# Stick-breaking steps of a hybrid block on one Trainium2 core: projection tiles placed ahead of the scores

## The chip, the cores and the metric

The kernel runs on one core of a Trainium2 chip. The metric is the device time of one execution, in microseconds (us). The kernel before the change took 1916.91 us, the median of three runs (1907.53 to 1917.92). The execution that was profiled took 1912.39 us.

A core has five engines that run their own instruction streams and meet at semaphores: PE (TensorE, matrix products; "PEld" is its weight loading), DVE (VectorE), ACT (ScalarE), POOL (GpSimd) and SP (SyncE, which here only starts transfers). An engine runs its instructions strictly in order, so an instruction that waits holds up all behind it.

## The reference, cut to what matters

The block normalises x, modulates it, and multiplies it by one wide projection matrix. The columns are split between a retention branch and a stick-breaking attention branch; both are merged, projected, and followed by a squared-ReLU MLP. The change is in the stick-breaking branch:

```python
def stick_breaking(q, k, v):
    scale = SB_DH ** -0.5
    for blk in range(S // SB_BLOCK):
        t0, t1 = blk * SB_BLOCK, (blk + 1) * SB_BLOCK
        z = jnp.einsum('bthd,bshd->bhts', q[:, t0:t1], k[:, :t1]) * scale
        valid = s_idx[None, :] < t_idx[:, None]
        log_1m = jnp.where(valid, -jax.nn.softplus(z), 0.0)
        log_stick = lax.cumsum(log_1m, axis=3, reverse=True) - log_1m
        a = jnp.where(valid, jnp.exp(jax.nn.log_sigmoid(z) + log_stick), 0.0)
        outs.append(jnp.einsum('bhts,bshd->bthd', a, v[:, :t1]))
```

S is 1024 and there are 8 heads of width 64. The kernel computes a as sigmoid(z) times a running product of sigmoid(-z), taken from the right.

## The kernel before, in words

All products are float32, each done as three passes over operands split into a high part (rounded) and a low part (the rest): high x high, high x low, low x high. The block runs in stages: normalisation (to about 74 us), the stick-breaking stage (about 74 to 388 us), gates, retention, merge, output projection and the MLP.

**Steps and units.** The stick-breaking stage is a written-out sequence of 48 steps, U = 0 to 47, in four groups G of 12 (two heads each); k is U modulo 12. A unit is up to four key blocks of 128 for one block of 128 queries (`UNITS`, line 72). Its width w is 128, 256, 384, 512 for k = 0 to 3, then 512 and 128, 512 and 256, 512 and 384, 512 and 512 for k = 4 to 11. Units that hold the diagonal (k = 0, 1, 2, 3, 4, 6, 8, 10) also get a mask product.

**What a unit passes through.** PE makes the scores S(U) (`scores`, lines 575 and 581). ACT makes four sigmoids from them (lines 944, 945: sigmoid(-z) into `uu`, sigmoid(z) into `sg`, for each head). DVE runs one scan for each head over `uu` (1297), at k = 4, 6, 8 and 10 a two-element copy (1300), and one product into `sg` (1303), after which the semaphore `a_done` says that the weights of unit U are ready. PE transposes them, WT(U) (`weights_transposed`, 591), ACT copies the result to `aT` (937), and PE multiplies by the values, V(U) (`times_v`, 608). WT(U) and V(U) stand in step U + 2, so the unit has until then to be ready.

**Tiles beside the steps.** The projections for q, k, v and the first gate columns are tiles 0 to 35 (`STICK_TILE`). Tiles 0 and 1 stand ahead of step 0, the others in steps by the table `STICK_BESIDE` (line 89), whole or in parts of their eight k chunks: a v tile, or half a q, k or gate tile, takes about 3 us. A line of it:

```python
    5: ((10, 0, 4),), 6: ((10, 4, 8),), 7: ((11, 0, 8),), 8: ((12, 0, 4),), 9: ((12, 4, 8),), 10: ((13, 0, 8),),
```

Steps 11, 23, 35 and 47 have no tile. A finished tile is evicted by ACT (`high`, lines 917, 920, 922); for q and k tiles DVE then makes the low part from the bank and the high part (`low`, 1278). A tile waits for the eviction of the tile two before it.

**Order on PE in one step:** WT(U-2), S(U), the tiles of the step, V(U-2). On ACT: the copy of a finished output block, the copy `aT`, the four sigmoids, then `high`. On DVE: scans, product, then `low`.

**Weights.** POOL splits each weight piece into high and low parts, two additions and two subtractions of 128x1024 (lines 410 and 412), into one of two slots. A piece can be split once the last tile that uses the slot's old piece has finished. In this stage these are tile 7 (in step 3), 13 (step 10), 15 (step 14), 23 (step 26), 29 (step 34), 31 (step 38) and 35 (step 46). Tile 16, in step 15, needs the piece whose split starts at the end of tile 15.

Of the kernel before, what the change touches and what calls it, by code (L numbers as in the profile page):

```python
# [12 lines left out]
KC = D // P  # L13
# [65 lines left out]
STICK_TILE = ([("q", 0, 0), ("k", 0, 0)] +  # L79
              [("v", 0, t) for t in range(4)] + [("q", 0, 1), ("k", 0, 1), ("v", 0, 4), ("v", 0, 5), ("q", 1, 0), ("v", 0, 6), ("k", 1, 0), ("v", 0, 7)] +  # L80
              [("q", 1, 1), ("k", 1, 1), ("v", 1, 0), ("q", 2, 0), ("v", 1, 1), ("k", 2, 0), ("v", 1, 2), ("v", 1, 3)] +
              [("q", 2, 1), ("k", 2, 1), ("v", 1, 4), ("v", 1, 5), ("q", 3, 0), ("v", 1, 6), ("k", 3, 0), ("v", 1, 7)] +
              [("q", 3, 1), ("k", 3, 1)] + [("a", 0, j) for j in range(4)])
# [62 lines left out]
def build_block(nc, x, wstream, ada, ada_rows, smalls, pos, ident, maskd, dprime, adab, postg, out, m1_dram, mods, x2_dram):  # L146
# [4 lines left out]
    with ctx:  # L151
# [3 lines left out]
        def sb(name, shape, dt, c=ctx):  # L155
            return c.enter_context(nc.sbuf_tensor(name, shape, dt))
# [65 lines left out]
        with ExitStack() as c:  # L222
            r_hi = sb("r_hi", [P, KC, S], f32r, c)
            r_lo = sb("r_lo", [P, KC, S], f32r, c)
            with ExitStack() as c2:
                qk = sb("qk", [P, T, 256], f32, c2)
# [265 lines left out]
        def _(pe):  # L492
# [63 lines left out]
            def passes(outp, hi, lo, r_hi_, r_lo_, start, stop):  # L556

                nc.tensor.matmul(outp, hi, r_hi_, start=start, stop=False)  # L558
                nc.tensor.matmul(outp, hi, r_lo_, start=False, stop=False)  # L559
                return nc.tensor.matmul(outp, lo, r_hi_, start=False, stop=stop)  # L560
# [22 lines left out]
            def weights_transposed(U):  # L583

                _, b0, b1, _ = UNITS[U % N_UNITS]
                pe.wait_ge(a_done, U + 1)
                if U:
                    pe.wait_ge(at_ready, U)
                for h in range(2):
                    for b in range(b1 - b0):  # L590
                        last = nc.tensor.transpose(px[:, h, b * P:(b + 1) * P], sg[:, U % 2, h, b * P:(b + 1) * P], id_f[:, :])  # L591
                last.then_inc(at_tr, 1)
# [21 lines left out]
            def stick_tile(n, k0=0, k1=KC):  # L614

                kind, at, tok = STICK_TILE[n]
                piece = 3 * (at // 2) + 2 * (at % 2) if kind in "qk" else 3 * at + 1 if kind == "v" else PC_GATE
                slot = piece % 2
                if k0 == 0:
                    pe.wait_ge(w_split, 4 * piece + 4)  # L620
                    if n == 0:
                        pe.wait_ge(n1_split, 16)
                    if n == TILE_AT["q", 0, 1]:
                        pe.wait_ge(n1_split, 32)
                    if n >= 4:
                        pe.wait_ge(*((ev_act, EA_STICK + n - 1) if STICK_TILE[n - 2][0] in "va" else (qk_low, LOW_AFTER[n - 1])))
                for k in range(k0, k1):
                    if kind == "v":
                        l, r_ = ((a[:, k, tok * P:(tok + 1) * P] for a in (a_hi, a_lo)), (w[:, slot, k * 256:(k + 1) * 256] for w in (w_hi, w_lo)))
                    else:  # L630
                        m, th = ("qk".index(kind), tok) if kind in "qk" else TT[tok]
                        l, r_ = ((w[:, slot, k * 256 + m * P:k * 256 + (m + 1) * P] for w in (w_hi, w_lo)),
                                 (a[:, k, th * HALF:(th + 1) * HALF] for a in (a_hi, a_lo)))
                    last = passes(tile_bank(n)[:, 0:256 if kind == "v" else HALF], *l, *r_, k == 0, k == KC - 1)
                if k1 == KC:
                    last.then_inc(gemm_done, 1)
# [3 lines left out]
            for U in range(ALL_UNITS + 2):  # L640
                if U >= 2:
                    weights_transposed(U - 2)
                if U < ALL_UNITS:
                    scores(U)
                for n, k0, k1 in STICK_BESIDE.get(U, ()):
                    stick_tile(n, k0, k1)
                if U >= 2:
                    times_v(U - 2)

# [7 lines left out]
            for g in range(GATE_G):  # L657
                ea, ev = EA_GATE + 8 * g, EV_GATE + 8 * g
                n = PC_GATE + 3 * g
# [225 lines left out]
        def _(act):  # L885
# [25 lines left out]
            def high(n):  # L911

                kind, at, tok = STICK_TILE[n]
                bank = tile_bank(n)
                act.wait_ge(gemm_done, TL_STICK + n + 1)
                if kind == "v":
                    nc.scalar.activation(vs[:, at, tok, :, :].rearrange("p a d -> p (a d)"), bank[:, 0:256], ACT.Copy).then_inc(ev_act, 1)
                elif kind == "a":
                    m, th = TT[tok]
                    nc.scalar.activation(m1s[:, m, th * HALF:(th + 1) * HALF], bank, ACT.Sigmoid).then_inc(ev_act, 1)  # L920
                else:
                    nc.scalar.activation(qk_hi[at % 2][:, "qk".index(kind), tok * HALF:(tok + 1) * HALF], bank, ACT.Copy,
                                         scale=SB_DH ** -0.5 if kind == "q" else 1.0).then_inc(ev_act, 1)
# [3 lines left out]
            for U in range(ALL_UNITS + 3):  # L927
                if U >= 3 and (U - 3) % N_UNITS in LAST_UNIT:
                    G, k = divmod(U - 3, N_UNITS)
                    i = UNITS[k][0]  # L930
                    act.wait_ge(av_done, T * G + i + 1)
                    nc.scalar.activation(sbt_f[:, G, i * P:(i + 1) * P], px[:, 2, 0:P], ACT.Copy).then_inc(sbt_ready, 1)
                if 2 <= U < ALL_UNITS + 2:
                    _, b0, b1, _ = UNITS[(U - 2) % N_UNITS]
                    w = (b1 - b0) * P
                    act.wait_ge(at_tr, U - 1)
                    nc.scalar.activation(aT[:, :, 0:w], px[:, 0:2, 0:w], ACT.Copy).then_inc(at_ready, 1)
                if U < ALL_UNITS:
                    _, b0, b1, _ = UNITS[U % N_UNITS]
                    w = (b1 - b0) * P  # L940
                    for h in range(2):
                        z = z_bank(2 * U + h, w)
                        act.wait_ge(z_done, 2 * U + h + 1)
                        nc.scalar.activation(uu[:, U % 2, h, HALF - w:HALF], z, ACT.Sigmoid, scale=-1.0).then_inc(sg_done, 1)  # L944
                        nc.scalar.activation(sg[:, U % 2, h, 0:w], z, ACT.Sigmoid).then_inc(sg_done, 1)
                for n, _, k1 in STICK_BESIDE.get(U, ()):
                    if k1 == KC:
                        high(n)

            def row_out(v):  # L950

# [253 lines left out]
        def _(dve):  # L1205
# [67 lines left out]
            def low(n):  # L1273

                kind, at, tok = STICK_TILE[n]
                m, cols = "qk".index(kind), slice(tok * HALF, (tok + 1) * HALF)
                dve.wait_ge(ev_act, EA_STICK + n + 1)
                V.scalar_tensor_tensor(qk_lo[at % 2][:, m, cols], tile_bank(n), 1.0 if m else SB_DH ** -0.5,
                                       qk_hi[at % 2][:, m, cols].bitcast(f32), ALU.mult, ALU.subtract).then_inc(qk_low, 1)
# [4 lines left out]
            for U in range(ALL_UNITS):  # L1284
                G, k = divmod(U, N_UNITS)
                _, b0, b1, diagonal = UNITS[k]
                w, slot = (b1 - b0) * P, U % 2
                pad = uu[:, slot, :, HALF:HALF + 1]
                if k == 1 and G:
                    V.memset(pad, 1.0).then_inc(pad_set, 1)  # L1290
                    pads += 1
                if pads:
                    dve.wait_ge(pad_set, pads)
                for h in range(2):
                    run = uu[:, slot, h, HALF - w:HALF if diagonal else HALF + 1][:, ::-1]
                    dve.wait_ge(sg_done, 4 * U + 2 * h + 1)
                    V.tensor_tensor_scan(run, run, run, 1.0, ALU.mult, ALU.bypass).then_inc(scan_done, 1)  # L1297
                dve.wait_ge(scan_done, 2 * U + 2)
                if k not in LAST_UNIT:
                    V.tensor_copy(uu[:, 1, :, HALF:HALF + 1], uu[:, 0, :, 0:1]).then_inc(pad_set, 1)  # L1300
                    pads += 1
                dve.wait_ge(sg_done, 4 * U + 4)
                V.tensor_tensor(sg[:, slot, :, 0:w], sg[:, slot, :, 0:w], uu[:, slot, :, HALF - w + 1:HALF + 1], ALU.mult).then_inc(a_done, 1)
                for n, _, k1 in STICK_BESIDE.get(U, ()):
                    if k1 == KC and STICK_TILE[n][0] in "qk":
                        low(n)


            dve.wait_ge(sbt_ready, 4 * T)
# [401 lines left out]
```

## Time and profile before

| | |
|---|---|
| median of three runs | 1916.91 us |
| profiled execution, time / span | 1912.39 / 1910.6 us |
| PE busy, share of the span | 1752.6 us, 92% |
| DVE busy | 952.9 us, 50% |
| ACT busy | 534.9 us, 28% |
| POOL busy | 667.9 us, 35% |
| PE in the chain that ended last | 82% |

The span is the time from the first to the last instruction of the profiled execution. Busy time is what an engine's instructions cover. The chain that ended last is followed back from the last instruction through what released each one. In rows of the trace, times are us from the start of the span; "[idle before <-X]" gives how long the engine stood idle ahead of a row and what ended it. "x8" is a number of merged instructions. The 48 steps cover 87 to 388 us. Where a matmul's bar overlaps the next one's, starts are what is to be read, since the ends are modelled.

### The profile page before, as it was taken

The numbers are of one execution on the slowest core, as the hardware profiler recorded it, in microseconds if no ns is written. First come the engines' busy times: TensorE is split into PE (matmuls) and PEld (weight loads), VectorE is DVE, ScalarE is ACT, GpSimd is POOL, SyncE is SP. The second block draws the span as 40 slices with busy tenths as digits, with TensorE's granted clock in tenths as the row PEclk, the third lists the DMA queues.
The fourth block names the chain that finished last, engine by engine and source line by source line (L and its number), as shares of the span: only waits on it lengthen the run. The fifth ranks groups of instructions, "written<-read, shape, count | busy, mean of one in ns | idle before, by whom it ended". The sixth has DMA issues, their size and how long they took to land.

```text
span 1910.6 us, 24819 instructions
## 1 busy us (share of the span) xinstructions
PE 1752.6 (92%) x9648; PEld 1449.9 (76%) x9648; DVE 952.9 (50%) x1291; ACT 534.9 (28%) x918; POOL 667.9 (35%) x282
## 2 busy tenths in 40 slices
PE   1697999899899989999999995789999999999998
PEld 1585777677698979897888895568888888888876
DVE  6647566766544554544111547464526345351616
ACT  3344454501012121211000233232333323233332
POOL 3014023214322313131334685055354444535320
PEclk8799999989899999999999997899999999999999
DMA  8001001146321111110311444111112021111213
GB/s 323 12 23 34 12 23 34 45 144 220 99 103 45 37 37 34 37 44 24 132 44 44 144 155 154 56 44 45 52 36 76 23 77 33 55 44 44 67 39 138
DMA packets 38076, 135.11 MB, mean 71 GB/s; under 512 B 5860, under 2 KB 6756, under 8 KB 37480
## 3 DMA queue, kind: packets, MB, share of 16 engines
q1 hardware_dynamic: 30304, 109.27, 17.1%
q10 hardware_dynamic: 7688, 24.67, 3.5%
q8 instruction: 59, 0.97, 0.2%
q14 instruction: 25, 0.20, 0.0%
HBM read 121.33 MB, written 12.60 MB: 70 GB/s over the span
## 4 chain that ended last, share of the span: by engine, by line
PE 82%; DVE 10%; issue 3%; POOL 2%; ACT 1%; DMA 0%; POOLq 0%; DVEq 0%; SPq 0%; ACTq 0%
PE ps L497 15%; PE ps L499 15%; PE ps L498 15%; PE ps L829 5%; PE ps L831 5%; PE ps L830 5%; PE ps L558 3%; PE ps L559 2%; PE ps L560 2%; PE ps L591 2%; PE ps L575 2%; PE ps L608 2%; PE ps L708 1%; DVE sg L1258 1%; DVE qk L1424 1%
## 5 line engine op out<-in xcount | busy, mean ns | idle before, releaser
L410 POOL TENSOR_TENSOR w_hi<-raw,zero 128x1024 fp32r<-128x1024 f32 x80 | 165.2, 2065 | 771.4 <-PE ps L499 371.0
L497 PE MATMUL ps<-r_hi,w_hi 128*128 128x512 f32 x640 | 253.6, 396 | 23.0 <-issue 20.3
L499 PE MATMUL ps<-r_hi,w_lo 128*128 128x512 f32 x640 | 254.9, 398 | 0.0
L498 PE MATMUL ps<-r_lo,w_hi 128*128 128x512 f32 x640 | 253.9, 397 | 0.0
L497 PE MATMUL ps<-w_hi,a_hi 128*128 128x256 f32 x768 | 225.4, 293 | 16.9 <-DVE qkT L1430 8.9
L499 PE MATMUL ps<-w_hi,a_lo 128*128 128x256 f32 x768 | 220.4, 287 | 0.0
L498 PE MATMUL ps<-w_lo,a_hi 128*128 128x256 f32 x768 | 220.3, 287 | 0.0
L412 POOL TENSOR_TENSOR w_lo<-raw,w_hi 128x1024 fp32r<-128x1024 f32 x80 | 210.6, 2632 | 6.3
L436 POOL TENSOR_TENSOR w_lo<-w,w_hi 128x1024 fp32r<-128x1024 f32 x39 | 99.6, 2553 | 251.6 <-ACT w_hi L1091 251.6
L1564 DVE TENSOR_TENSOR m<-m,ps 128x512 f32<-128x512 f32 x224 | 146.2, 682 | 71.3 <-PE ps L831 70.8
L497 PEld LDWEIGHTS ps<-w_hi,a_hi 128*128 128x128 f32 x768 | 150.1, 195 | 21.1 <-POOL w_hi L410 10.1
L829 PE MATMUL ps<-w_hi,f_hi 128*128 128x512 f32 x392 | 156.3, 399 | 5.8 <-issue 4.7
L497 PEld LDWEIGHTS ps<-r_hi,w_hi 128*128 128x128 f32 x640 | 120.9, 189 | 52.6 <-issue 20.5
L1297 DVE TENSOR_TENSOR_SCAN uu<-uu 128x512 f32<-128x512 f32 (+7 forms) x96 | 108.9, 1175 | 100.0 <-ACT uu L944 100.0
L830 PE MATMUL ps<-w_lo,f_hi 128*128 128x512 f32 x392 | 155.9, 398 | 0.0
L831 PE MATMUL ps<-w_hi,f_lo 128*128 128x512 f32 x392 | 155.9, 398 | 0.0
L498 PEld LDWEIGHTS ps<-w_lo,a_hi 128*128 128x128 f32 x768 | 150.2, 196 | 0.0
L499 PEld LDWEIGHTS ps<-w_hi,a_lo 128*128 128x128 f32 x768 | 149.8, 195 | 0.0
L498 PEld LDWEIGHTS ps<-r_lo,w_hi 128*128 128x128 f32 x640 | 120.9, 189 | 30.2
L499 PEld LDWEIGHTS ps<-r_hi,w_lo 128*128 128x128 f32 x640 | 121.0, 189 | 28.9
L1557 DVE TENSOR_TENSOR f_lo<-hid,f_hi 128x1024 fp32r<-128x1024 f32 x35 | 51.7, 1478 | 150.2 <-ACT f_hi L1118 150.2
L436 POOL TENSOR_TENSOR w_lo<-raw,w_hi 128x1024 fp32r<-128x1024 f32 x32 | 77.6, 2432 | 102.0 <-ACT w_hi L1091 101.6
(224 smaller groups left out, 3369.4 us busy)
## 6 DMA issues: line engine op xcount, KB each, us to landing
raw<-wstream SPq DMA_DIRECT2D x112, 512.0 KB, 3.6
ada_r<-ada_rows SPq DMA_DIRECT2D x32, 512.0 KB, 4.6
w<-wstream SPq DMA_DIRECT2D x32, 512.0 KB, 3.5
ada_s<-ada SPq DMA_DIRECT2D x8, 1024.0 KB, 18.5
xs<-x SPq DMA_DIRECT2D x2, 2048.0 KB, 11.0
m_dram<-m1s ACTq DMA_DIRECT2D x1, 4096.0 KB, 13.0
m<-m_dram ACTq DMA_DIRECT2D x1, 4096.0 KB, 12.5
x_dram<-m ACTq DMA_DIRECT2D x8, 512.0 KB, 2.9
```

Of the source, the lines that this page charges most:

```text
L410: nc.gpsimd.tensor_tensor(w_hi[:, slot, part], raw[:, h, :], zero[:, 0:1].broadcast_to([P, RAW]), ALU.add).then_inc(w_split, 1)
L412: nc.gpsimd.tensor_tensor(w_lo[:, slot, part], raw[:, h, :], w_hi[:, slot, part].bitcast(f32), ALU.subtract).then_inc(w_split, 1)
L436: return nc.gpsimd.tensor_tensor(out_, in0, in1, op)
L497: nc.tensor.matmul(outp, lh, rh, start=(k == 0), stop=False)
L498: nc.tensor.matmul(outp, lh, rl, start=False, stop=False)
L499: last = nc.tensor.matmul(outp, ll, rh, start=False, stop=(k == chunks - 1))
L558: nc.tensor.matmul(outp, hi, r_hi_, start=start, stop=False)
L829: nc.tensor.matmul(banks[:, t, :], fh, wh, start=(start and c == 0), stop=False, skip_group_check=not start)
L830: nc.tensor.matmul(banks[:, t, :], fh, wl, start=False, stop=False, skip_group_check=not start)
L831: last = nc.tensor.matmul(banks[:, t, :], fl, wh, start=False, stop=(c == 1), skip_group_check=not start)
L1297: V.tensor_tensor_scan(run, run, run, 1.0, ALU.mult, ALU.bypass).then_inc(scan_done, 1)
L1564: V.tensor_tensor(dst, dst, bank, op).then_inc(ff_ev, 1)
```

## The change

In each step, PE now runs the step's tiles ahead of the scores instead of behind them; ACT evicts a finished tile ahead of the step's sigmoids; DVE makes the low part of a q or k tile ahead of the step's scans. Nothing else is changed: the table, the buffers, the waits and the number of instructions are the same. Lines below the edits shift by three on DVE (1297 is 1300 after the change, 1303 is 1306, while 1278 stays) and on ACT (944 is 947, 945 is 948).

```diff
             for U in range(ALL_UNITS + 2):
                 if U >= 2:
                     weights_transposed(U - 2)
+                for n, k0, k1 in STICK_BESIDE.get(U, ()):
+                    stick_tile(n, k0, k1)
                 if U < ALL_UNITS:
                     scores(U)
-                for n, k0, k1 in STICK_BESIDE.get(U, ()):
-                    stick_tile(n, k0, k1)
                 if U >= 2:
                     times_v(U - 2)
...
                     nc.scalar.activation(aT[:, :, 0:w], px[:, 0:2, 0:w], ACT.Copy).then_inc(at_ready, 1)
+                for n, _, k1 in STICK_BESIDE.get(U, ()):
+                    if k1 == KC:
+                        high(n)
                 if U < ALL_UNITS:
...
                         nc.scalar.activation(sg[:, U % 2, h, 0:w], z, ACT.Sigmoid).then_inc(sg_done, 1)
-                for n, _, k1 in STICK_BESIDE.get(U, ()):
-                    if k1 == KC:
-                        high(n)
...
                 _, b0, b1, diagonal = UNITS[k]
+                for n, _, k1 in STICK_BESIDE.get(U, ()):
+                    if k1 == KC and STICK_TILE[n][0] in "qk":
+                        low(n)
...
                 V.tensor_tensor(sg[:, slot, :, 0:w], sg[:, slot, :, 0:w], uu[:, slot, :, HALF - w + 1:HALF + 1], ALU.mult).then_inc(a_done, 1)
-                for n, _, k1 in STICK_BESIDE.get(U, ()):
-                    if k1 == KC and STICK_TILE[n][0] in "qk":
-                        low(n)
```

PE in step 10, before the change, from WT(8) to the start of step 11: L591 are the transposes of the weights, L575 and L581 the scores of unit 10 with their mask, L558 the first pass of each k chunk of tile 13, L608 the product with v.

```order
L591 MATMUL ps<-id_f,sg 128x128 [waits at_ready,a_done]
...
L575 MATMUL ps<-qk_hi0 128x512 [waits sg_done]
...
L581 MATMUL ps<-msk_b,id_b 128x128 x2
L558 MATMUL ps<-w_hi,a_hi 128x256 [waits ev_act,w_split]
...
L608 MATMUL ps<-aT,vs 64x128 [waits sbt_ready,ev_act,at_ready]
L608 MATMUL ps<-aT,vs 64x128 x7
```

The same step after the change:

```order
L591 MATMUL ps<-id_f,sg 128x128 [waits at_ready,a_done]
...
L558 MATMUL ps<-w_hi,a_hi 128x256 [waits ev_act,w_split]
...
L575 MATMUL ps<-qk_hi0 128x512 [waits sg_done]
...
L581 MATMUL ps<-msk_b,id_b 128x128 x2
L608 MATMUL ps<-aT,vs 64x128 [waits sbt_ready,ev_act,at_ready]
L608 MATMUL ps<-aT,vs 64x128 x7
```

The scores have moved behind the 24 matmuls of the tile, and nothing stands between them and V(8) now.

DVE in steps 9 and 10 before the change, from the first scan of unit 9 (384 wide, with one carried element) to the product of unit 10; L1278 is the low part of tile 12, a k tile that ends in step 9.

```order
L1297 SCALAR_TENSOR_TENSOR uu<-uu 128x385 [waits sg_done,pad_set]
L1297 SCALAR_TENSOR_TENSOR uu<-uu 128x385 [waits sg_done]
L1303 TENSOR_TENSOR sg<-sg,uu 128x2x384 [waits sg_done,scan_done]
L1278 SCALAR_TENSOR_TENSOR qk_lo<-ps,qk_hi 128x512 [waits ev_act]
L1297 SCALAR_TENSOR_TENSOR uu<-uu 128x512 [waits sg_done,pad_set]
L1297 SCALAR_TENSOR_TENSOR uu<-uu 128x512 [waits sg_done]
L1300 COPY uu<-uu 128x2 [waits scan_done]
L1303 TENSOR_TENSOR sg<-sg,uu 128x1024 [waits sg_done]
```

The same place after the change:

```order
L1278 SCALAR_TENSOR_TENSOR qk_lo<-ps,qk_hi 128x512 [waits ev_act]
L1300 SCALAR_TENSOR_TENSOR uu<-uu 128x385 [waits sg_done,pad_set]
L1300 SCALAR_TENSOR_TENSOR uu<-uu 128x385 [waits sg_done]
L1306 TENSOR_TENSOR sg<-sg,uu 128x2x384 [waits sg_done,scan_done]
L1300 SCALAR_TENSOR_TENSOR uu<-uu 128x512 [waits sg_done,pad_set]
L1300 SCALAR_TENSOR_TENSOR uu<-uu 128x512 [waits sg_done]
L1303 COPY uu<-uu 128x2 [waits scan_done]
L1306 TENSOR_TENSOR sg<-sg,uu 128x1024 [waits sg_done]
```

The low part has moved from behind the product of unit 9 to ahead of its scans.

## Rows read from the trace of the kernel before

**Rows 1.** Waits of PE, 86 to 392 us: total us, times, longest us.

```profile
PE ps L591 <- DVE sg L1303: 11.6, 5, 5.4
PE ps L558 <- POOL w_lo L412: 8.4, 1, 8.4
PE ps L608 <- ACT aT L937: 2.4, 2, 1.3
PE ps L575 <- DVE qk_lo L1278: 1.4, 1, 1.4
```

**Rows 2.** Windows, a stretch without long waits: length, busy us, PE clock, DMA.

```profile
240.00:300.00 60.00, 59.50 (x444) 46.30 (x443) 37.74 (x43) 31.89 (x71) 10.26 (x4) 1.00 0.06 19
```

**Rows 3.** Chain, steps 22 to 24: S(22), V(20), WT(22); start us, us.

```profile
231.51 0.90 PE ps L575 x4
...
235.49 1.02 PE ps L608 x16
...
239.10 1.02 PE ps L591 x8
```

**Rows 4.** Chain: the scores S(16), 512 wide.

```profile
198.92 0.89 PE ps L575 x6
```

**Rows 5.** Timeline of DVE behind these scores: start us, us, instruction, idle before.

```profile
200.71 2.34 DVE L1297 TENSOR_TENSOR_SCAN uu<-uu 128x512 f32<-128x512 f32 x2 [7.45 <-ACT uu L944]
...
203.16 1.22 DVE L1303 TENSOR_TENSOR sg<-sg,uu 128x1024 f32<-128x1024 f32 x1
```

**Rows 6.** Timeline of POOL: weight splits after tiles 7, 13, 23 and 35.

```profile
115.00 1.89 POOL L410 TENSOR_TENSOR w_hi<-raw,zero 128x1024 fp32r<-128x1024 f32 x1 [64.13 <-PE ps L560]
...
155.87 1.89 POOL L410 TENSOR_TENSOR w_hi<-raw,zero 128x1024 fp32r<-128x1024 f32 x1 [31.43 <-PE ps L560]
157.84 3.30 POOL L412 TENSOR_TENSOR w_lo<-raw,w_hi 128x1024 fp32r<-128x1024 f32 x1
161.10 2.81 POOL L410 TENSOR_TENSOR w_hi<-raw,zero 128x1024 fp32r<-128x1024 f32 x1
163.99 3.15 POOL L412 TENSOR_TENSOR w_lo<-raw,w_hi 128x1024 fp32r<-128x1024 f32 x1
...
257.43 1.89 POOL L410 TENSOR_TENSOR w_hi<-raw,zero 128x1024 fp32r<-128x1024 f32 x1 [65.25 <-PE ps L560]
...
370.40 1.90 POOL L410 TENSOR_TENSOR w_hi<-raw,zero 128x1024 fp32r<-128x1024 f32 x1 [33.07 <-PE ps L560]
```

**Rows 7.** Timeline of DVE during the split after tile 13.

```profile
155.93 1.85 DVE L1300 COPY uu<-uu 128x2 f32<-128x2 f32 x1
157.70 1.21 DVE L1303 TENSOR_TENSOR sg<-sg,uu 128x1024 f32<-128x1024 f32 x1
159.24 5.75 DVE L1297 TENSOR_TENSOR_SCAN uu<-uu 128x513 f32<-128x513 f32 x2 [0.33 <-ACT uu L944]
165.03 3.19 DVE L1303 TENSOR_TENSOR sg<-sg,uu 128x1024 f32<-128x1024 f32 x1
```

**Rows 8.** Chain: WT(3), WT(11), WT(27), and the first gate matmul.

```profile
123.96 1.02 PE ps L591 x8
...
168.27 1.09 PE ps L591 x8
...
268.99 1.09 PE ps L591 x8
...
387.85 0.73 PE ps L497
```

**Rows 9.** Windows around waits of PE: the granted clock is third from the end.

```profile
170.00:172.00 2.00, 2.00 (x7) 1.61 (x6) 1.20 (x2) 1.53 (x5) 0.00 (x0) 0.50 0.03 12
172.00:174.00 2.00, 2.00 (x8) 1.58 (x7) 0.77 (x2) 0.14 (x1) 0.00 (x0) 0.69 0.00 0
...
194.00:196.00 2.00, 2.00 (x11) 2.00 (x11) 0.00 (x0) 0.00 (x0) 0.00 (x0) 0.50 0.43 174
...
270.00:272.00 2.00, 2.00 (x13) 1.65 (x13) 1.97 (x4) 1.70 (x5) 0.00 (x0) 1.00 0.30 121
```

## The prediction

> **What bounds the kernel now.** I read the waits of PE in the stick-breaking stage first, then one quiet stretch, then the chain and the timelines of DVE and POOL around the longest waits. In the quiet stretch PE is busy 59.5 of 60 us at full clock, DVE 37.7 and ACT 31.9 [rows 2]: PE's own work sets the pace, and reordering gains nothing there unless a handover gets shorter. All of PE's other time is in four kinds of wait [rows 1]: 11.6 us for unit weights (`a_done`), 8.4 us once for a weight split, 2.4 us for the copy `aT`, and 1.4 us ahead of S(0) for the low part of tile 1. So the change can win at most 23.8 us here, and the question is what it does to each.
>
> The largest kind is made by POOL. Unhindered, scores that start at 198.92 have their first scan at 200.71 and the product's end at 204.38: 1.8 us and 5.5 us after the start of S [rows 4, 5]. During a split it is another picture [rows 6, 7]. A two-element copy takes 1.85 us and ends with POOL's first operation. POOL's next one takes 3.30 us, and it ends 2.2 us after DVE's product has ended (158.91 to 161.14). The second scan ends at 164.99, 1.1 us after POOL's third operation (163.91); the last product ends at 168.22, 1.1 us after the fourth (167.14). The two engines take turns, operation by operation: 1.9 and 2.2 us for POOL, 1.1 to 1.2 us for a 512-wide scan or product.
>
> Read instead as plain slowing (5.75 + 3.19 us for what takes 2.34 + 1.22), unit 10 below would be ready at T+10.7 and not T+9.5, and each of six events dearer by up to 1.2 us; I go by turns, and this is in the range.
>
> The Trainium skill (SBUF — State Buffer, section "SBUF: two separate sides") says of these two engines that the port pair they share is an exclusive lock, kept for a whole instruction, and no split of bandwidth. By that rule the sum is the one below, by plain slowing some 7 us more. The trace agrees with the rule: the waits end where the other engine's operations end.
>
> **The change part by part.** It removes and adds no instruction and no DMA; POOL's and SP's orders stay. What changes is distance. WT(U) needs the product of unit U. Before, S(U) had its own tile, V(U-2), WT(U-1), S(U+1), the tile of step U+1 and V(U-1) behind it to cover its 5.5 us. Now its own tile is ahead of it, so the cover is one tile, about 3.0 us, shorter: V(20) starts 4.0 us after S(22), 1.0 of scores and 3.0 of tile [rows 3]. Second, a split starts when a tile ends. Before, the scores of that step were already out by then; now the scores come after, so all DVE work of that unit falls into the split. T is the end of the tile that lets a split start; the new T is earlier than the old by the scores that moved behind it (1.0 us for 512 wide, 0.8 for 384).
>
> *Quiet steps.* With a tile in the next step the cover is 6.3 us or more (for k = 6: 1.0 + 1.0 + 0.4 + 3.0 + 0.5 + 0.4, phase lengths scaled from [rows 3] by the number of blocks), against 5.5: nothing is lost. Unit 22 has no tile in step 23. From S(22) to WT(22) are 7.6 us now, of which the tile was 3.0 [rows 3]; left are 4.6 against 5.5, so +0.9 us. Units 10, 34 and 46 have no such tile either, but meet a split.
>
> *Split after tile 13 (T = 155.8), unit 10.* S(10) starts at T, its scan is ready at T+1.8, and POOL's first operation ends at T+2.0 [rows 6]. By turns: scan to 3.1, POOL to 5.3, scan to 6.4, POOL to 8.3, copy and product to 9.5, POOL to 11.7. PE has only 4.6 us of work (same widths as unit 22), so WT(10) waits 4.9 us. Then WT(10), five chunks of tile 14, S(12), V(10) are 1.0 + 3.7 + 0.6 + 1.1 = 6.4, and WT(11) starts at T+15.9; the product of unit 11 ends at 11.7 + 1.1 + 1.2 + 1.2 = T+15.2, in time. The new T is 1.0 earlier: 14.9, against 168.27 - 155.8 = 12.5 now [rows 8]. That is +2.4. The split after tile 29 (unit 34) has the same widths: +2.4.
>
> *Splits after tiles 23 and 31 (T = 257.35), units 26 and 38, 384 wide.* Scan and product cost 0.9 (three quarters of [rows 5]): 2.0, 2.9, 5.1, 6.0, 7.9, product at T+8.8. PE has 0.8 + 0.4 + 0.6 + 3.0 + 1.0 + 0.6 = 6.4, so it waits 2.4. Then 5.6 more to WT(27), T+14.4, less 0.8 is 13.6, against 268.99 - 257.35 = 11.6 now [rows 8]: +2.0 each.
>
> *Split after tile 7 (T = 114.95), unit 3.* Tile 8 still stands between, so the scan is ready at T+4.8. POOL ends its third operation at 6.2 first; scan 7.3, POOL 9.5, scan 10.6, product 11.8 (POOL is done). Less 1.0 is 10.8, against 123.96 - 114.95 = 9.0 [rows 8]: +1.8, with 1.7 us idle.
>
> *Split after tile 15.* Tile 16 waits for it before and after [rows 1]. Before, S(14) and S(15) were both out ahead of that wait; now only S(14) is, and S(15) (1.0) stands behind tile 16. One more DVE operation gets in among POOL's (0.9), and the start is 0.8 earlier: +1.0 rounded.
>
> *End, split after tile 35 (T = 370.3), units 46 and 47.* As for unit 10, the product of 46 is at T+9.5 and that of 47 at T+15.2. WT(47) at the low clock 2.0, `aT` 1.1, V(47) 2.0 give T+20.3, less 1.0 is 19.3, against 387.85 - 370.3 = 17.5 [rows 8]: +1.8.
>
> *Start.* Tiles 2 and 3 now stand where PE waited for the low part of tile 1: -1.4 [rows 1]. `high` and `low` ahead of sigmoids and scans cost nothing: they run (0.6 and 0.7 us on ACT and DVE, estimated from the 128x512 scan and product of [rows 5]) while PE makes the scores that the sigmoids wait for. Without that cover each would cost its own length in a step that waits, 6 x 0.7 = 4.2 us at most, which I keep for the range.
>
> *Clock.* After the wait of 2.58 us that ends with WT(11) at 168.27 the granted clock is 0.50 and then 0.69 in the next windows, 1.2 instead of 2.4 GHz for some 3 us: about 1.5 us lost. After the 8.4 us wait it is 0.50 still two to four us on. After the 0.5 us wait ahead of WT(27) it stays 1.00 [rows 9]. So the two 2.4 us waits add 1.5 each; the 4.9 us waits of units 10 and 34 add 2.0 where 1.5 is paid already, +0.5 each; the 1.7 us wait of unit 3 lies between 0 and 1.5, and I take 0. Clock: +4.0.
>
> *Handovers.* PE changes kind of work four times a step before and after, but tile to scores and scores to V are pairs that the quiet trace hardly shows. Over 44 steps with a tile, bounds are -0.1 and +0.1 us a step, -4.4 and +4.4; I take 0, since each of the present four handovers costs about the same.
>
> Sum: 0.9 + 2.4 + 2.4 + 2.0 + 2.0 + 1.8 + 1.0 + 1.8 - 1.4 + 4.0 = +16.9 us. All later stages start from the end of this one and are untouched, so it reaches the end. The profiled execution took 1912.4 us: 1929.3. The median of the three runs is 4.5 us higher; from it the sum gives 1933.8. I say 1932.
>
> **Rivals.**
> *Relocation only.* POOL's and DVE's work during a split is fixed, so the new wait at unit U may just replace the old one at U+1, and each event costs only the moved scores. For it: after the first unit the next one's product (T+15.2) does come in time. Against: PE's remaining work behind WT(10) is 6.4 us, and it can't run during the wait. It would give about 6 x 1.0 + 0.9 - 1.4 = +5.5, 1921.
> *More clock and dearer handovers.* If the clock falls after the 1.7 us wait too (+1.5), if the handovers cost 0.1 more (+4.4) and `high` and `low` delay the sigmoids (+4.2): +27, 1942. For it: scores use half of the array's rows, and leaving a tile for them is a change of shape; against: nothing in the trace shows a dear one.
> *Faster, by the handovers.* If V right behind the scores, and the tile right behind the transposes, start without a gap, a quiet step gets shorter. The chip would have to give back over 16.9 / 44 = 0.38 us a step to break even, and 0.6 to be 0.5% faster. With half of the 1.0 us of the scores hidden, 0.5 a step, it is -22 + 16.9 = -5, 1910. Against: PE is busy 59.5 of 60 us in such steps [rows 2].
>
> **How the numbers follow.** The forecast has 0.68, relocation 0.14, the dearer case 0.13, the faster one 0.05. The forecast's own range is 1925 to 1939: the handovers' bounds and 3 us of spread between runs. To hold 8 in 10 the range goes from 1921 to 1941. This kernel's measurement tells about 0.5%, 9.6 us, from no change, so slower begins at 1926.5. The forecast puts nearly all of its chance there, the dearer case all, relocation a little: slower 0.83. Same is most of relocation, part of the faster case and the low end of the forecast: 0.14. Faster 0.03.
>
> **What would show it.** In the changed profile the waits of PE for the product (now line 1306) should be about 25 us in seven or eight waits instead of five: near 4.9 at WT(10) and WT(34), 2.4 at WT(26) and WT(38), 1.7 at WT(3), 0.9 at WT(22), and those at WT(11) and WT(35) gone. The wait for the low part ahead of S(0) should be gone, the one for the split of tile 16 about 9 us. The first gate matmul should start near 388 + 17 = 405 us. Clock windows of 0.50 should follow four waits that have none now or a shorter one. I am wrong if WT(10) waits under 3 us, if a quiet step is over 0.1 us longer or shorter than now, or if a stage after the first gate matmul differs by over 2 us in length.

## The result and the profile after

The changed kernel takes 1917.85 us, the median of 20 runs (1915.67 to 1920.13). The kernel before, now with 20 runs, the three from before the change among them, takes 1909.28 us (1902.99 to 1917.92). The ratio is 1.004, with a 95% interval of 1.0028 to 1.0053: slower by 8.6 us, clear of no change but under the 9.6 us from which I had called a result slower. I had forecast 1932 us in a range of 1921 to 1941. The measured time lies 3 us below that range: the sign was right, the shift of the stage was forecast twice too large (16.9 us against 8.0).

The waits of PE in the stage, changed kernel (total us, times, longest us), to be set against [rows 1]:

```profile
PE ps L591 <- DVE sg L1306: 20.2, 8, 4.4
PE ps L558 <- POOL w_lo L412: 8.6, 1, 8.6
PE ps L608 <- ACT aT L937: 2.2, 2, 1.1
```

The waits for unit weights grew from 11.6 us in five to 20.2 us in eight; the wait ahead of S(0) is gone; that for tile 16 is as before. PE's timeline in the changed kernel shows where the eight lie (start us, us, instruction, idle before): WT(3), WT(10), WT(22), WT(26), WT(34), WT(38), WT(46) and WT(47).

```profile
124.22 1.09 PE L591 MATMUL ps<-id_f,sg 128*128 128x128 f32 x8 [1.80 <-DVE sg L1306]
...
163.42 1.97 PE L591 MATMUL ps<-id_f,sg 128*128 128x128 f32 x8 [4.39 <-DVE sg L1306]
...
240.47 1.09 PE L591 MATMUL ps<-id_f,sg 128*128 128x128 f32 x8 [0.72 <-DVE sg L1306]
...
266.02 0.87 PE L591 MATMUL ps<-id_f,sg 128*128 128x128 f32 x6 [1.89 <-DVE sg L1306]
...
310.92 1.97 PE L591 MATMUL ps<-id_f,sg 128*128 128x128 f32 x8 [4.39 <-DVE sg L1306]
...
339.10 0.87 PE L591 MATMUL ps<-id_f,sg 128*128 128x128 f32 x6 [1.95 <-DVE sg L1306]
...
385.30 1.97 PE L591 MATMUL ps<-id_f,sg 128*128 128x128 f32 x8 [4.40 <-DVE sg L1306]
...
390.97 1.97 PE L591 MATMUL ps<-id_f,sg 128*128 128x128 f32 x8 [0.61 <-DVE sg L1306]
```

Before the change the five waits were at WT(11) and WT(35) (2.6 us each), WT(27) and WT(39) (0.5 each) and WT(47) (5.4). At unit 22 no split runs, and the scans are as short as ever; only the cover is shorter. In the other places a split runs, and a scan starts only when POOL's operation has ended. The timelines of POOL and DVE in the changed kernel during the split after tile 13, to be set against [rows 6, 7]:

```profile
154.31 1.89 POOL L410 TENSOR_TENSOR w_hi<-raw,zero 128x1024 fp32r<-128x1024 f32 x1 [32.48 <-PE ps L560]
156.28 3.17 POOL L412 TENSOR_TENSOR w_lo<-raw,w_hi 128x1024 fp32r<-128x1024 f32 x1
159.41 2.81 POOL L410 TENSOR_TENSOR w_hi<-raw,zero 128x1024 fp32r<-128x1024 f32 x1
162.29 3.29 POOL L412 TENSOR_TENSOR w_lo<-raw,w_hi 128x1024 fp32r<-128x1024 f32 x1
```

```profile
156.03 4.50 DVE L1300 TENSOR_TENSOR_SCAN uu<-uu 128x512 f32<-128x512 f32 x2 [2.84 <-ACT uu L947]
160.56 1.68 DVE L1303 COPY uu<-uu 128x2 f32<-128x2 f32 x1
162.15 1.21 DVE L1306 TENSOR_TENSOR sg<-sg,uu 128x1024 f32<-128x1024 f32 x1
```

The whole DVE work of unit 10 now lies in the split, operation against operation: scans done at 160.53, POOL's third operation at 162.22, copy behind it, product at 163.36. The tile had ended at 154.2, so the product is ready 9.2 us later; I had worked out 9.5.

**Where the time went.** When WT(U-2) starts in step U, PE has done the same work in both orders, so the starts in the two timelines can be subtracted. The first tile starts 0.1 us later in the changed kernel, which is taken off in the first line.

| stretch | measured shift, us | forecast, us |
|---|---|---|
| start, to WT(0) (100.21 to 98.80) | -1.5 | -1.4 |
| split after tile 7, to WT(3) | +1.9 | +1.8 |
| split after tile 13, WT(9) to WT(12) | +1.6 | +2.9 |
| split after tile 15 | +0.1 | +1.0 |
| unit 22 | +0.9 | +0.9 |
| split after tile 23, WT(25) to WT(27) | +1.5 | +3.5 |
| split after tile 29, WT(33) to WT(36) | +3.0 | +2.9 |
| split after tile 31, WT(37) to WT(39) | +2.9 | +3.5 |
| end, WT(45) to the first gate matmul | +1.3 | +1.8 |
| all other steps | -3.5 | 0 |
| first gate matmul, 387.8 to 396.0 | +8.2; without the late start +8.0 | +16.9 |

The shift of the stage, 8.0 us, accounts for nearly all of the difference of the medians (8.6). The two profiled spans differ by only 3.5 us, and this needs a word. Retention, between the first and the last of its gate matmuls, took 315.0 us in the profiled execution of before and 311.6 in that of the changed kernel (window, length, busy us, clock), before and after:

```profile
569.10:884.10 315.00, 299.98 (x2049) 269.58 (x2048) 154.78 (x410) 54.65 (x118) 84.06 (x40) 0.97 0.11 36
```

```profile
576.30:887.90 311.60, 296.43 (x2049) 266.01 (x2048) 154.78 (x410) 54.68 (x118) 84.07 (x40) 0.98 0.12 36
```

DVE, ACT and POOL do the same in both, PE has as many instructions, and the clock was 0.01 lower. I take that for chance of a run and not for the change: in twelve of the fourteen profiles below that stretch took 311.0 to 311.7 us, in the old and in the new order of the stage alike; the other two, both with a new order on PE, took 312.3 and 314.7.

### The profile page after: what moved, and what is told of

Same layout as the page of the kernel before. It is cut to its first block, busy times and chain, and to the rows that moved or that the text cites. A ratio compares the mean times of both kernels' runs of the same rounds, so it can differ in the third digit from the quotient of the medians.

```text
span 1914.1 us, 24819 instructions
## 1 busy us (share of the span) xinstructions
PE 1748.2 (91%) x9648; PEld 1449.0 (76%) x9648; DVE 952.0 (50%) x1291; ACT 531.6 (28%) x918; POOL 667.8 (35%) x282
## 4 chain that ended last, share of the span: by engine, by line
PE 81%; DVE 11%; issue 3%; POOL 2%; ACT 1%; DMA 0%; POOLq 0%; DVEq 0%; SPq 0%; ACTq 0%
PE ps L497 15%; PE ps L498 15%; PE ps L499 15%; PE ps L829 5%; PE ps L831 5%; PE ps L830 5%; PE ps L558 3%; PE ps L559 3%; PE ps L560 3%; PE ps L591 2%; DVE uu L1300 2%; PE ps L575 1%; PE ps L608 1%; PE ps L708 1%; DVE sg L1258 1%
## 5 line engine op out<-in xcount | busy, mean ns | idle before, releaser
L497 PE MATMUL ps<-r_hi,w_hi 128*128 128x512 f32 x640 | 253.0, 395 | 22.8 <-issue 20.2
L1300 DVE TENSOR_TENSOR_SCAN uu<-uu 128x512 f32<-128x512 f32 (+7 forms) x96 | 115.1, 1240 | 81.9 <-ACT uu L947 81.5
```

The lines of the kernel that those rows point to most:

```text
L497: nc.tensor.matmul(outp, lh, rh, start=(k == 0), stop=False)
```

## The experiments

Each kernel is timed beside the kernel before on the same chip. The shift given is that of the first gate matmul against 387.8 us. It is read from one profiled execution of each kernel and holds the chance of its start: where the clock was low during the first tiles, at 74 to 78 us, all that follows came up to 1.3 us later.

**The new order in the quiet steps, and in the split steps.** A set of steps selects the order in all three streams:

```diff
+SPLIT_STEPS = (3, 10, 14, 22, 26, 34, 38, 46)
...
-                for n, k0, k1 in STICK_BESIDE.get(U, ()):
-                    stick_tile(n, k0, k1)
+                if U not in SPLIT_STEPS:
+                    for n, k0, k1 in STICK_BESIDE.get(U, ()):
+                        stick_tile(n, k0, k1)
                 if U < ALL_UNITS:
                     scores(U)
+                if not (U not in SPLIT_STEPS):
+                    for n, k0, k1 in STICK_BESIDE.get(U, ()):
+                        stick_tile(n, k0, k1)
```

The second run has `U in SPLIT_STEPS` in its place. ACT's and DVE's streams are edited in the same way.

> The new order in all steps except 3, 10, 14, 22, 26, 34, 38 and 46 (those where a weight split starts, and 22, whose next step has no tile), which keep the old order. Theory A (the loss is made in the split steps by the shorter cover, while all other steps gain about 0.1 us each by cheaper handovers and the start 1.5 us): none of the new waits, first gate matmul 1.5 + 36 x 0.1 = 5 us earlier than before, near 383 us, and the time 0.2 to 0.3% under before. Rival B (the new order costs in every step, the waits only happen to lie in the split steps): first gate matmul at or after 388 us, time 0 to 0.3% over before.

> The complement: the new order only in steps 3, 10, 14, 22, 26, 34, 38 and 46. Theory A: all of the new waits (20 us for the product instead of 11.6), no start gain, nearly no handover gain: first gate matmul 12 to 13 us later than before, near 400 us, time 0.6 to 0.7% over before, that is over the changed kernel too. Rival B: under half of that, 4 us or less. If the two parts are independent, the shifts of this run and of the run with the other steps add up to the 8.2 us of the full change.

Measured: quiet steps only, 1903.71 us, ratio 0.9974 (0.9957 to 0.9991), shift -3.3. Split steps only, 1921.57 us, ratio 1.0072 (1.005 to 1.0094), shift +15.4. The waits of PE for the product, quiet and split:

```profile
PE ps L592 <- DVE sg L1317: 12.6, 5, 5.4
```

```profile
PE ps L592 <- DVE sg L1317: 20.0, 8, 4.4
```

The loss is made in eight steps, and the other 36 with a tile bring time: 3.3 us, where I had said 5. The two shifts add to 12.1, not 8.2. Two parts of the difference can be named: their starts to WT(0) are 1.7 us later together than that of the full change, by the clock of the first tiles; and in the split-steps run the clock fell behind the wait of WT(26), which cost 2.9 us where the full change lost 1.5:

```profile
270.00:272.00 2.00, 1.12 (x6) 0.84 (x6) 2.00 (x2) 0.00 (x0) 1.92 (x2) 0.81 0.16 64
272.00:274.00 2.00, 2.00 (x10) 1.21 (x10) 2.00 (x1) 0.86 (x2) 1.04 (x1) 0.50 0.00 0
```

**POOL taken out of the stage, both orders.** The splits of pieces 2 to 8 cover 32 columns in place of 1024. These two kernels leave out the other columns of those weights' high and low parts, so they do not compute the block; they show only what the time is without POOL's work.

```diff
-                    part = slice(h * RAW, (h + 1) * RAW)
+                    part = slice(h * RAW, h * RAW + width)
...
-                piece(n, n + 1, n % 2, TL_STICK + TILE_AT[last] + 1)
+                piece(n, n + 1, n % 2, TL_STICK + TILE_AT[last] + 1, 32)
```

> Old order, but the weight splits of pieces 2 to 8 cover 32 of 1024 columns only (the low and high parts of those pieces are left out otherwise), so POOL is gone from the stage while all semaphores stay. Theory A: the waits of PE for the product and for the split vanish (11.6 and 8.4 us), the low clock behind them too (some 5 us): first gate matmul near 361 to 365 us. Rival B (the scans are slow by themselves, POOL has little to do with it): the waits for the product stay over 5 us.

> New order with the same narrow splits. Theory A: without POOL the shorter cover costs only 0.9 us each at units 10, 22, 34 and 46, against 1.5 us at the start and 0.1 us a step of handovers: first gate matmul 1 to 3 us earlier than in the old order with narrow splits, so that the sign of the change turns. Rival B (the order itself costs): 3 us or more later.

Measured: old order 1880.58 us, shift -26.6; new order 1877.45 us, shift -28.5. Without the splits the new order is 1.9 us earlier, 1.5 of them at the start: the sign of the change turns. The old order has no wait for the product left (its 2.4 us for `aT` and 1.4 us ahead of S(0) stay); the new one has five short ones:

```profile
PE ps L591 <- DVE sg L1306: 3.1, 5, 0.7
```

So the splits cost this stage 26.6 us in the old order, most of it in the two kinds of wait of [rows 1] that are gone (11.6 and 8.4 us), the rest in the low clock behind them: PE's busy time in the stage fell from 278.0 to 271.2 us, with the clock at 1.00 and not 0.96.

**The low clock behind a wait.** The changed kernel with unused matmuls ahead of WT(10) and WT(34). The line left out waits until the bank that they write is free:

```diff
+                if U in (12, 36):
...
+                    for _ in range(18):
+                        nc.tensor.matmul(tile_bank(14), a_hi[:, 0, 0:P], a_hi[:, 0, 0:HALF], start=True, stop=True)
                 if U >= 2:
                     weights_transposed(U - 2)
```

> The changed kernel with 18 unused matmuls (128x512, into the free bank of the next tile) ahead of WT(10) and ahead of WT(34), where PE waits 4.4 us. Theory A (part of what a wait costs is the low clock after it): the granted clock stays at 1.00 through both places, WT and the tile behind it take 0.85 and 3.7 us instead of 1.6 and 4.3 to 5.5, and the first gate matmul comes 3 to 4 us earlier than in the changed kernel, near 392 us. Rival B (the clock follows something else): no change, or 1 us later.

Measured: 1912.16 us, ratio 1.0019 (0.9998 to 1.0041), shift +5.3, 2.8 less than the changed kernel. From WT(9) to WT(12) it lost 0.3 us and not 1.6, from WT(33) to WT(36) 0.3 and not 3.0: 4.0 us in these two places; 1.3 were lost at the start of the stage, before the first edit, by the clock of the first tiles. Windows behind WT(10), in the changed kernel and in this one:

```profile
163.00:165.00 2.00, 1.58 (x8) 1.58 (x9) 2.00 (x2) 0.00 (x0) 2.00 (x1) 0.51 0.00 0
165.00:167.00 2.00, 2.00 (x8) 1.63 (x7) 2.00 (x2) 1.02 (x1) 0.58 (x1) 0.64 0.24 29
```

```profile
164.00:166.00 2.00, 1.90 (x13) 1.39 (x13) 2.00 (x2) 0.10 (x1) 2.00 (x1) 1.00 0.00 0
166.00:168.00 2.00, 2.00 (x10) 1.62 (x9) 2.00 (x2) 0.92 (x1) 0.95 (x1) 1.00 0.11 12
```

WT(10) came as long after WT(9) as in the changed kernel (to 0.03 us); only the clock held. Theory A stands, with 4.0 us in the two places where I had said 3 to 4.

**The two halves of the change apart.**

> Only PE's part of the change: tiles ahead of scores, while ACT evicts behind the sigmoids and DVE makes low parts behind the product, as before. Theory A: as the changed kernel, except that the low part of tile 7 now stands behind the product of unit 3, which the split delays, and S(4) waits for it, about 3 us more: first gate matmul near 399 us. Rival C (evicting ahead of the sigmoids is what costs in the changed kernel): 3 us or more earlier than the changed kernel.

> Only the part of ACT and DVE: the tile stands behind the scores on PE as before, but is evicted ahead of the sigmoids. Theory A: the sigmoids of a step in which a tile ends now wait for its end, so the cover is a tile shorter as in the changed kernel, with none of its gains at the handovers: waits of PE for the product 20 to 27 us, first gate matmul 12 to 17 us later than before. Rival C: as before within 2 us.

The first has only the first hunk of the diff, the second only the others. Measured: PE's part alone 1929.2 us, ratio 1.0109 (1.0072 to 1.0145), shift +18.6; ACT's and DVE's part alone 1940.58 us, ratio 1.0169 (1.0132 to 1.0207), shift +30.9. Waits of PE in the first:

```profile
PE ps L591 <- DVE sg L1307: 17.0, 7, 4.1
...
PE ps L558 <- DVE qk_lo L1282: 7.2, 1, 7.2
```

and in the second:

```profile
PE ps L591 <- DVE sg L1312: 23.5, 8, 5.2
...
PE ps L575 <- ACT sg L949: 5.8, 9, 2.2
```

Both directions were right and both shifts too small: I had said some 11 us and 12 to 17. In the first it was not S(4) that waited for the low part of tile 7 but tile 9, which needs the bank of tile 7 and now stands ahead of S(4): 7.2 us, where I had said 3. PE also waited 2.6 us for evictions of v tiles. In the second, PE also waited for the sigmoids themselves, 5.8 us, which I had left out: they free the banks of the scores. The largest part that I had left out is the clock. Windows of the stage, before and in the second kernel:

```profile
86.00:387.80 301.80, 277.97 (x2033) 216.61 (x2033) 182.34 (x178) 142.66 (x307) 73.25 (x28) 0.96 0.08 27
```

```profile
86.00:418.60 332.60, 289.50 (x2038) 224.51 (x2036) 182.57 (x178) 135.47 (x307) 74.25 (x28) 0.92 0.07 25
```

PE is busy 11.5 us longer with the same work, at a clock of 0.92 (third from the end) and not 0.96; in the changed kernel it was 0.7 us longer, at 0.94.

Rival C is out: with tiles ahead on PE, evicting ahead of the sigmoids saves time.

**A third order: the scores first.**

```diff
+                if U == 0:
+                    for n, k0, k1 in STICK_BESIDE[0]:
+                        stick_tile(n, k0, k1)
+                if U < ALL_UNITS:
+                    scores(U)
                 if U >= 2:
                     weights_transposed(U - 2)
-                if U < ALL_UNITS:
-                    scores(U)
...
```

The part left out keeps step 0's tiles from standing twice on PE, and moves ACT's eviction of tiles 2 and 3 ahead of the sigmoids of unit 0. In the second run the scores stand first only in steps with a tile.

> A third order: S(U), WT(U-2), tile, V(U-2), with tiles 2 and 3 ahead of S(0); ACT and DVE as before. Theory A: the product has two tiles of cover again (5.5 us and about 5.6 us to spare with the sigmoids behind the copy aT), so the waits in the split steps are those of before, while the pair transposes to tile and the start keep their gain: first gate matmul 4 to 5 us earlier than before, near 383 us, time 0.2 to 0.3% under before. Rival D (the handover gain belongs to scores directly ahead of V): first gate matmul at 386 to 388 us.

> As the run with the scores first, but in the steps without a tile (11, 23, 35, 47) PE keeps transposes, scores, product with v. Theory A: the waits for the copy aT in those steps go (about 1.1 us each), all else stays: first gate matmul 6 to 9 us earlier than before, time 0.3 to 0.4% under before. Rival: the waits only change their name, within 1 us of the run with scores first.

Measured: 1904.12 us, ratio 0.9984 (0.9965 to 1.0002), shift -5.3; and 1904.81 us, ratio 0.9981 (0.9963 to 1.0), shift -7.0. The waits for the product are 9.9 and 12.2 us, about as before the change (11.6); those for `aT` fell from 5.9 to 2.2 by the second edit. The stage moved as theory A has it, and rival D (386 to 388 us) is out, the first gate matmul being at 382.5; the times can't tell these two from the kernel before with certainty, nor from each other.

**Shorter splits.** ACT makes the high parts of pieces 2 to 8 behind the sigmoids and `high`, POOL only the low parts.

```diff
+            def weights_high(n, last):
+                act.wait_ge(gemm_done, TL_STICK + last + 1)
+                for h in range(2):
+                    act.wait_ge(raw_full[h], 16 * (n + 1))
+                    nc.scalar.activation(w_hi[:, n % 2, h * RAW:(h + 1) * RAW], raw[:, h, :], ACT.Copy).then_inc(w_act, 1)
...
+                if U in WEIGHTS_AT:
+                    weights_high(*WEIGHTS_AT[U])
```

> Old order, but ACT makes the high parts of weight pieces 2 to 8, so that POOL has only the two subtractions left in each split. Theory A: a split takes some 6.5 us instead of 11.3, so the wait for tile 16 falls from 8.4 to about 4 us and the waits for the product by more than half, the low clock with them: first gate matmul 10 to 14 us earlier than before. Rival (ACT is then late with its sigmoids, 2 us of added work in such a step): 5 us or less.

> The changed kernel's order with the same shorter splits. Theory A (the sign of the change depends on the length of the splits, which its shorter cover meets): the 8.2 us by which it is later now shrink to between 0 and 4 us against the old order with the same splits. Rival B: 8 us as before.

Measured: old order 1892.77 us, ratio 0.9925 (0.9901 to 0.9948), shift -14.3. New order 1906.92 us, ratio 0.9981 (0.9959 to 1.0003), shift -4.9. The old order did nearly as expected: one wait for the product of 2.3 us is left, and tile 16 waits 5.3, where I had said 4. The new order stays 9.5 us behind it, where I had said 0 to 4: rival B's number came (8), and what the new order costs did not shrink with the splits. Its waits:

```profile
PE ps L566 <- POOL w_lo L408: 9.5, 2, 7.0
PE ps L616 <- ACT aT L952: 8.1, 5, 2.0
PE ps L599 <- DVE sg L1323: 4.1, 5, 2.1
```

In the old order with the same splits these are 5.3, 3.5 and 2.3 us. The three together are 10.6 us longer in the new order; less the wait of 1.4 us at the start, that is 9.2 of the 9.5. My reason for it was that ACT's high parts stood behind sigmoids that now come late. The next run moves them ahead of the sigmoids:

> The changed order with ACT's high parts of the weights directly behind the eviction of the tile, ahead of the step's sigmoids, and not behind them as in the run before. Theory A (in that run the high parts stood behind sigmoids that now wait for the later scores, so each split began some 3 us late and tile 16 waited 7.0 us instead of 5.3): the splits start at the tile's end again, the wait for tile 16 is 5 us or less, the one of 2.5 us for the piece of tile 10 goes, and the first gate matmul comes 3 to 7 us earlier than in that run, 7 to 12 us before that of the unchanged kernel. Rival (the shorter cover itself costs as much with shorter splits): within 2 us of that run, and the time moves into waits for the product, over 8 us of them.

Measured: 1916.14 us, ratio 1.0045 (1.0024 to 1.0065), shift +12.5. The first half came true, the second didn't:

```profile
PE ps L599 <- DVE sg L1323: 19.3, 7, 3.7
PE ps L566 <- POOL w_lo L408: 5.2, 1, 5.2
```

The splits began in time and the waits of tiles for them fell from 9.5 to 5.2 us, but ACT's two operations now delay the sigmoids of seven units and come back as waits for the product. Neither theory had this right: in the new order nothing is left in a split step to hide about 2 us on ACT, ahead of the sigmoids or behind them. That this alone makes the 9.5 us is argued, not shown; with the splits taken out altogether, and ACT's work as it was, the new order was the earlier one.

**The best versions.**

> Scores first in steps with a tile, together with ACT's high parts. Theory A: the two gains add up: first gate matmul 16 to 22 us earlier than before, time 0.8 to 1.2% under before. Rival: ACT's added work delays the sigmoids, which already stand behind the copy aT here, and under 12 us are left.

> New order except in steps 3, 10, 14, 22, 26, 34, 38 and 46, with ACT's high parts behind the sigmoids. Theory A: the gain of that order (3.3 us with a start 0.4 us late) and that of the shorter splits (14.3 us) add up: first gate matmul 17 to 19 us earlier than before, time 0.8 to 1.1% under before. Rival: ACT's added work in a step with the eviction elsewhere delays the copy aT, 14 us or less.

Measured: scores first with ACT's high parts 1892.68 us, ratio 0.9916 (0.9888 to 0.9943), shift -19.6; the new order in the quiet steps, the old one in the split steps, with ACT's high parts 1890.62 us, ratio 0.9904 (0.9877 to 0.9931), shift -18.9. Waits of the latter:

```profile
PE ps L567 <- POOL w_lo L409: 5.5, 1, 5.5
PE ps L617 <- ACT aT L957: 3.5, 5, 1.1
PE ps L600 <- DVE sg L1334: 2.3, 1, 2.3
```

Both beat the kernel before and the changed one, and in the second the gains add up to within 1.3 us: -14.3 and -3.3 give -17.6, against -18.9. Against the old order with ACT's high parts alone (1892.77 us) the stage is 5.3 and 4.6 us shorter, but the times, 0.1 and 2.2 us lower with ranges that overlap, don't show it with certainty.

## Why the prediction was right in sign and wrong in size

The mechanism held and the sum did not: it gave +16.9 us where the stage moved by 8.0. The step that failed is the sizing of its terms: the handovers, put at nothing, were -3.5 us; the waits behind the splits were 3.1 us shorter than worked out; the clock was 1.3 and the split after tile 15 was 0.9 less than charged. By the bound that I had set, 9.6 us from no change, the measured 8.6 us counts as "same", to which I had given 0.14, and not as "slower", to which I had given 0.83.

*The cover.* Right. A unit's own tile left its cover, the waits appeared at the units that were named, WT(11) and WT(35) lost theirs, and without splits the change gains (the narrow pair). What the shorter cover costs with half-length splits I had wrong (the 9.5 us above).

*Turns between POOL and DVE.* Right. The product of unit 10 was due 9.5 us after the tile and came at 9.2. Plain slowing would have given 10.7. The waits of 4.9, 2.4, 1.7 and, without a split, 0.9 were 4.4, 1.9, 1.8 and 0.7.

*Handovers, set to 0 between -4.4 and +4.4.* This is the largest term that failed: -3.5 us over the other steps. The chain of the kernel before shows V(14), WT(15), S(17), tile, V(15):

```profile
202.88 0.81 PE ps L608 x12
203.69 1.02 PE ps L591 x8
204.71 0.48 PE ps L575 x6
205.19 0.44 PE ps L558
...
208.21 1.02 PE ps L608 x16
```

and that of the changed kernel V(14), WT(15), tile, S(17), V(15):

```profile
204.10 0.81 PE ps L608 x12
204.91 1.02 PE ps L591 x8
...
208.73 0.48 PE ps L575 x6
209.21 1.02 PE ps L608 x16
```

The same work takes 5.33 us before and 5.11 after. In the timelines the eight transposes hand over after 1.02 us to scores and after 0.85 us to a tile. Scores with a mask ahead of V take 1.12 us where they took 1.00 ahead of a tile, so a step with a 512-wide diagonal unit gains nearly nothing and one without a mask 0.2. I had taken 0 because the four present handovers cost about the same; the new pairs don't. The bound of -4.4 held it, the value I chose did not.

*The clock, set to +4.0.* Behind the waits of WT(10) and WT(34) the tile took 4.3 and 5.5 us in place of 3.7; behind WT(26) nothing was lost, behind WT(38) 1.5. Windows of the changed kernel:

```profile
266.00:268.00 2.00, 1.98 (x17) 1.98 (x18) 2.00 (x1) 0.81 (x1) 2.00 (x1) 1.00 0.00 0
268.00:270.00 2.00, 2.00 (x17) 1.84 (x18) 2.00 (x2) 0.21 (x1) 0.20 (x1) 1.00 0.40 70
...
341.00:343.00 2.00, 2.00 (x6) 1.57 (x5) 2.00 (x2) 0.00 (x0) 0.27 (x1) 0.50 0.28 63
```

Two waits of 1.9 us with the same kinds of work in front, one with the clock at 1.00 behind it and one at 0.50. (Behind the first stands a v tile, behind the second half a gate tile; but behind the first the clock fell as well in the split-steps run.) I had charged 1.5 to each. Net of what before paid, the clock cost about 2.7 us (-0.1, +1.3 and +1.5), 1.3 less than forecast.

*The split after tile 15, set to +1.0.* It cost 0.1. I had added a third DVE operation of 0.9 us to POOL's turns; the split took 10.3 us in both kernels, since the 384-wide operations that meet it now are shorter than the 512-wide ones that met it before.

*Shorter waits than worked out* make up the rest: 0.5 to 0.7 us in each of five splits, 3.1 us together, the cheaper handovers within them included. *The start* (-1.4 forecast, -1.5 measured) was right.

*The base.* The 1932 us are the sum laid over 1915.1, between the profiled execution (1912.39) and the median of three runs (1916.91); twenty runs give 1909.28. Of the 14.2 us between 1932 and 1917.85, 8.3 are the sum (16.9 against the measured 8.6), the other 5.9 the base. With either error alone, a range of the same width would have held the measured time.

*Rivals.* Relocation only would have had +5.5; the measured +8.6 lies between it and the forecast, but the loss does not come in steps of 1.0 us a split: it is 0.1 to 3.0. The dearer case is out: behind the 1.8 us wait of unit 3 the clock stayed at 1.00, `high` and `low` added no wait, and of the handovers only that of masked scores to V was dearer. The faster case was right about the tile behind the transposes and wrong about V behind masked scores; the handovers gave 3.5 / 44 = 0.08 us a step where it needed 0.38.

*The signs that I had named.* WT(10) waited 4.4 us and not under 3. The first gate matmul started at 396.0 and not near 405. The clock fell behind WT(10), WT(34) and WT(38), not behind WT(26). Two of the signs of being wrong came: a quiet step without a mask is 0.2 us shorter, which is the failed term of the handovers, and retention differs by 3.4 us, which I take for chance of a run.

## What to carry to other kernels

When work is moved ahead of the start of a chain that another engine must finish, count the cover that each link has left, above all where something else slows that chain: eight steps of 48 made the whole loss here. An order can be chosen for each step; new order where the cover is ample and old order where it is not beat both (1903.71 us). And when two engines take turns at a resource, shortening the one's part can be worth more than a reordering: 14 us here against 3 to 7.

## What the runs showed of the hardware that was not expected

- PE's handovers between kinds of matmul differ by pair: transposes to a 128-row tile 0.17 us cheaper than to 64-row scores; masked scores to the 64-column product with v 0.12 us dearer than to a tile.
- After a PE wait of 1.9 us the granted clock held in one place (WT(26)) and fell in another (WT(38)) of the same execution; in another kernel it fell behind WT(26) too (270 to 274 us above). 18 unused matmuls in a 4.4 us wait kept it at 1.00 and saved 1.3 and 2.7 us.
- The kernel before ranges over 15 us between runs, and its mean clock goes with it: in one group of 27 runs, 1903.0 us at 0.968 and 1918.9 us at 0.957. The median of the first three runs lay 7.6 us above that of twenty.
